# Output projections with tokens on partitions, and norms handed on in pieces of one and two k-tiles

## The reference

```python
def layer_norm(x, g, b):
    mu = jnp.mean(xf, axis=-1, keepdims=True)
    var = jnp.mean(jnp.square(xf - mu), axis=-1, keepdims=True)
    return (xf - mu) * lax.rsqrt(var + LN_EPS) * g + b
...
        x = layer_norm(ALPHA * x + mix, ln1_g[layer], ln1_b[layer])            # mix = ... @ w_out
        x = layer_norm(ALPHA * x + conv_ffn(x, ...), ln2_g[layer], ln2_b[layer])  # ... @ w_down
...
        h = rms_norm_2(x, ln_pre_g[layer])
        proj = jnp.einsum('bsd,de->bse', h, w_in[layer])
...
        y = jnp.einsum('bsd,de->bse', merged, w_o[layer])
        x = x + rms_norm_2(y, ln_post_g[layer])
```

## Time and profile before

| | |
|---|---|
| median of 3 runs | 3606.42 us (3606.31 to 3611.41) |
| profiled execution, its own time | 3607.19 us |
| its span (first to last instruction) | 3605.3 us |
| TensorE matmuls, share of the span | 3450.6 us, 96% |
| DVE, ACT, POOL | 64%, 40%, 11% |
| granted TensorE clock, mean | 0.985 of full |

### The profile page before, as it was taken

The page is one execution under the profiler, slowest core; times in us unless marked ns, Lnnn a source line. Parts: engine busy times, 40 slices in busy tenths (PEclk is TensorE's granted clock), DMA queues, the critical chain, the costliest instruction groups (busy, mean ns, idle before and its releaser), DMA issues.

```text
span 3605.3 us, 48876 instructions
## 1 busy us (share of the span) xinstructions
PE 3450.6 (96%) x19568; PEld 2980.7 (83%) x19568; DVE 2311.8 (64%) x2199; ACT 1428.3 (40%) x1113; POOL 405.9 (11%) x240
## 2 busy tenths in 40 slices
PE   8999899999999999899999999989999899999997
PEld 7888788888888888688888888878788788788886
DVE  5754667788874466467888874458766556545666
ACT  5542344333333345444333333345533333343332
POOL 0400130111111101030111111100000000000002
PEclk9999899999999999999999999999999999999999
DMA  5444144554555544144555455534444434435543
GB/s 209 172 175 145 71 161 175 186 184 179 184 186 187 186 146 172 59 164 168 182 185 186 179 183 192 187 131 155 162 177 181 145 140 175 152 134 185 183 179 135
DMA packets 84065, 598.16 MB, mean 166 GB/s; under 512 B 9329, under 2 KB 10481, under 8 KB 12146
## 3 DMA queue, kind: packets, MB, share of 16 engines
q1 hardware_dynamic: 81216, 589.34, 45.3%
q10 hardware_dynamic: 2738, 7.23, 0.6%
HBM read 594.43 MB, written 2.10 MB: 165 GB/s over the span
## 4 chain that ended last, share of the span: by engine, by line
PE 66%; issue 19%; DVE 7%; ACT 3%; POOLq 2%; POOL 1%; DVEq 1%; DMA 0%; ACTq 0%
PE acc L263 38%; PE acc L262 20%; DVE w_lo L192 4%; PE acc L259 3%; ACT w_hi L188 2%; POOLq L346 2%; PE acc L260 1%; PE acc L1431 1%; POOL over L344 1%; PE acc L1482 0%; DVE u_tiles L283 0%; PE acc L360 0%; PE acc L386 0%; DVE over L283 0%; POOLq L730 0%
## 5 line engine op out<-in xcount | busy, mean ns | idle before, releaser
L263 PE MATMUL acc<-x_hi_lo,w_hi 128*128 128x512 f32 x6720 | 2367.9, 396 | 0.0
L192 DVE TENSOR_TENSOR w_lo<-w_raw,w_hi 128x2048 fp32r<-128x2048 f32 x560 | 1387.6, 2478 | 1096.5 <-ACT w_hi L188 1095.1
L262 PE MATMUL acc<-x_hi_lo,w_lo 128*128 128x256 f32 x6720 | 1894.8, 282 | 15.5 <-DVE w_lo L192 15.5
L188 ACT ACTIVATE w_hi<-w_raw 128x2048 fp32r<-128x2048 f32 x560 | 1073.0, 1916 | 1963.2 <-PE acc L263 1963.2
L263 PEld LDWEIGHTS acc<-x_hi_lo,w_hi 128*128 128x128 f32 x6720 | 1266.1, 188 | 297.6 <-issue 4.1
L262 PEld LDWEIGHTS acc<-x_hi_lo,w_lo 128*128 128x128 f32 x6720 | 1273.0, 189 | 31.1 <-DVE w_lo L192 12.2
L263 PE MATMUL acc<-hidden_hi_lo,w_hi 128*128 128x512 f32 x1728 | 604.4, 395 | 0.0
L262 PE MATMUL acc<-hidden_hi_lo,w_lo 128*128 128x256 f32 x1728 | 482.2, 279 | 3.5 <-DVE w_lo L192 3.5
L263 PEld LDWEIGHTS acc<-hidden_hi_lo,w_hi 128*128 128x128 f32 x1728 | 324.2, 188 | 76.3
L262 PEld LDWEIGHTS acc<-hidden_hi_lo,w_lo 128*128 128x128 f32 x1728 | 325.3, 188 | 5.2 <-DVE w_lo L192 4.4
L259 PE MATMUL acc<-x_hi_lo,w_hi 128*128 128x512 f32 x448 | 169.1, 410 | 48.0 <-DVE w_lo L192 32.7
(11 more groups left out here) (250 smaller groups left out, 1685.7 us busy)
## 6 DMA issues: line engine op xcount, KB each, us to landing
w_raw<-weights_dram SPq DMA_DIRECT2D x560, 1024.0 KB, 4.8
resid<-x_dram ACTq DMA_DIRECT2D x4, 512.0 KB, 10.3
over<-w_gates_dram ACTq DMA_DIRECT2D x1, 2048.0 KB, 7.4
out_dram<-resid SPq DMA_DIRECT2D x4, 512.0 KB, 2.7
over<-con_dram ACTq DMA_DIRECT2D x5, 128.0 KB, 2.4
par<-par_dram ACTq DMA_DIRECT2D x1, 525.0 KB, 12.2
over<-con_dram ACTq DMA_DIRECT2D x2, 256.0 KB, 7.3
over<-gmlp_ws_dram ACTq DMA_DIRECT2D x1, 512.0 KB
```

What stands on the lines that cost most here:

```text
L188: nc.scalar.activation(whi[:, slot, :], raw[:, slot, :], ACT.Copy).then_inc(weights_hi, 1)
L192: nc.vector.tensor_tensor(wlo[:, slot, :], raw[:, slot, :], whi[:, slot, :].bitcast(F32), ALU.subtract).then_inc(weights_split, 1)
L262: nc.tensor.matmul(*rest, start=False, stop=False)
L263: last = nc.tensor.matmul(*both, start=False, stop=(k == CK * nch - 1))
```

## The change

In the five stages of `BY_TOKEN` the roles in the product are exchanged (`multiply_by_token`): a block of 128 tokens of the activations is loaded, hi or lo, and the weights stream past it, 512 output columns at a time, so that a bank holds 128 tokens by 512 features. Three matmuls of 512 columns (hi x hi, hi x lo, lo x hi) take the place of two pairs. A task uses two banks, one for each block `b` of tokens; in its last chunk all of block 0 comes first and is announced by `block_done`. The residual is kept token-major too (`z`: 128 x 2 x 2048), x is loaded a second time in that form, and gain and bias of the norms come as rows written to all partitions (`load_row`). Moments of a token are then sums along the free axis: `bn_stats` for each 512 features, `bn_aggr` at the end, a root on ACT for one column and a reciprocal. The affine step is two scalar_tensor_tensor on the DVE. The next stage needs feature-major input: TensorE transposes pieces (`GROUPS`: two of one k-tile and seven of two) into PSUM banks 4 to 7, ACT makes the hi part from there, the DVE the lo part, and TensorE waits for each piece by itself within the first task (`turn_before`). POOL no longer takes part in the norms. In last_out ACT squares the banks with an accumulated sum, the DVE multiplies by the gain row, and at the end one operation scales and adds for each 512 features, stored in eight parts. Since pieces of the norm run on ACT and the DVE, the split of the next stage's second chunk is moved to behind group 3 (`hold`).

```diff
+GROUPS = [(0,), (1,)] + [(k, k + 1) for k in range(2, MT, 2)]
+NGROUP = len(GROUPS)
...
+BY_TOKEN = ("mix0_out", "down0", "attn_out", "down1", "last_out")
+BLOCK0 = {n: 4 * i for i, n in enumerate(BY_TOKEN)}
+FEEDS = {"mix0_out": ("up0", 0), "down0": ("attn_in", 1), "attn_out": ("up1", 2), "down1": ("rnn_in", 3)}
...
-                            if not isinstance(n, int) or n + 2 < NCHUNKS:
+                            if not (last and hold) and (not isinstance(n, int) or n + 2 < NCHUNKS):
...
+                            if first and c < nch - 1 and f == 0:
+                                before_k(k)
...
+        def multiply_by_token(pe, name, moving, ready=None, cuts=(), banks_read=None):
...
+                        if c < nch - 1:
+                            places = [(b, kk) for kk in range(CK) for b in range(2)]
+                        else:
+                            places = [(b, kk) for b in range(2) for kk in range(CK)]
+                        for b, kk in places:
+                            bank, k = 4 * t + b, CK * c + kk
+                            w_hi, w_lo = (w[:, s, kk * CF * P:(kk + 1) * CF * P] for w in (whi, wlo))
+                            x_hi_b, x_lo_b = (moving(k, at0 + b * P, at0 + (b + 1) * P) for at0 in (0, T))
+                            nc.tensor.matmul(acc[:, bank, :], x_hi_b, w_hi, start=(k == 0), stop=False)
+                            nc.tensor.matmul(acc[:, bank, :], x_hi_b, w_lo, start=False, stop=False)
+                            last = nc.tensor.matmul(acc[:, bank, :], x_lo_b, w_hi, start=False,
+                                                    stop=(k == CK * nch - 1))
+                            if k == CK * nch - 1 and b == 0:
+                                last.then_inc(block_done, 1)
+                        last.then_inc(chunk_used, 1)
...
+        def wait_block(eng, name, q, b, n):
+            if b == 0:
+                eng.wait_ge(block_done, BLOCK0[name] + q + 1)
+            else:
+                eng.wait_ge(chunk_used, n + 1)
...
+        def affine(dve, b, at0, n):
+            zp = part(b, at0, n)
+            dve.scalar_tensor_tensor(zp, zp, moments[:, b, 0:1], row_g[:, at0:at0 + n], ALU.subtract, ALU.mult)
+            dve.drain()
+            return dve.scalar_tensor_tensor(zp, zp, rst[:, b:b + 1], row_b[:, at0:at0 + n], ALU.mult, ALU.add)
...
+        def group_scale(dve, g):
+            at0, n = group_cols(g)
+            for b in range(2):
+                o = dve.scalar_tensor_tensor(u_tok[:, b, at0:at0 + n], part(b, at0, n), rst[:, b:b + 1],
+                                             pre_row[:, at0:at0 + n], ALU.mult, ALU.mult)
+            o.then_inc(x_tok, 1)
...
+        def dve_residual(name):
...
+                for b in range(2):
+                    zp = part(b, 512 * q, 512)
+                    wait_block(dve, name, q, b, n)
+                    o = dve.scalar_tensor_tensor(zp, zp, ALPHA, acc[:, 4 * t + b, :], ALU.mult, ALU.add)
+                    if b:
+                        o.then_inc(acc_free, 1)
+                    dve.drain()
+                    dve.bn_stats(stats[:, b, q, :], zp)
+                    if q == 3:
+                        dve.drain()
+                        dve.bn_aggr(moments[:, b, :], stats[:, b].rearrange("p q s -> p (q s)")).then_inc(ln_var, 1)
+                        if b == 0:
+                            dve.wait_ge(rows_landed, 16 * (2 * occ + 2))
+                        dve_rstd(dve, 2 * occ + b + 1, b)
+                        if name == "down1":
+                            dve_pre_affine(dve, b)
+                        elif b == 0:
+                            affine(dve, 0, *group_cols(0))
+                        else:
+                            affine(dve, 1, *group_cols(0)).then_inc(x_tok, 1)
...
+        def dve_pre_affine(dve, b):
             for q in range(4):
+                affine(dve, b, 512 * q, 512).then_inc(z_norm, 1)
...
+        def group_lo(dve, nxt, g):
+            k0, n = GROUPS[g][0], len(GROUPS[g])
+            dve.wait_ge(x_hi, READY0[nxt] + g + 1)
+            dst = xhl[:, k0:k0 + n, :]
+            dve.tensor_tensor(dst[:, :, T:2 * T], acc[:, 4 + g % 4, 0:n * T].rearrange("p (k n) -> p k n", k=n),
+                              dst[:, :, 0:T].bitcast(F32), ALU.subtract).then_inc(moving_ready, 1)
+        def group_hi(act, nxt, g):
+            k0, n = GROUPS[g][0], len(GROUPS[g])
+            act.wait_ge(turned, NGROUP * FED_BY[nxt][1] + g + 1)
+            act.activation(xhl[:, k0:k0 + n, 0:T], acc[:, 4 + g % 4, 0:n * T].rearrange("p (k n) -> p k n", k=n),
+                           ACT.Copy).then_inc(x_hi, 1)
+        def group_turn(pe, nxt, g):
+            occ = FED_BY[nxt][1]
+            src = u_tok if nxt == "rnn_in" else z
+            pe.wait_ge(x_tok, NGROUP * occ + g + 1)
+            for at0, k in enumerate(GROUPS[g]):
+                for b in range(2):
+                    o = pe.transpose(acc[:, 4 + g % 4, at0 * T + b * P:at0 * T + (b + 1) * P],
+                                     src[:, b, k * P:(k + 1) * P], ident[:])
+            o.then_inc(turned, 1)
+        def turn_before(pe, nxt):
+            def before_k(k):
+                for g, ks in enumerate(GROUPS):
+                    if ks[0] == k:
+                        if g + 1 < NGROUP:
+                            group_turn(pe, nxt, g + 1)
+                        pe.wait_ge(moving_ready, READY0[nxt] + g + 1)
+            return before_k
+        def norm_pe(pe, nxt):
+            keep_clock(pe, 24)
+            group_turn(pe, nxt, 0)
+        def norm_dve(dve, name):
+            nxt = FEEDS[name][0]
+            go = group_affine
+            if name == "down1":
+                dve.wait_ge(pre_landed, 16)
+                dve.wait_ge(squares, 8)
+                dve.tensor_reduce(moments[:, :, 0], parts[:], AX, ALU.add).then_inc(ln_var, 1)
+                dve_rstd(dve, 9, 0, 2)
+                go = group_scale
+                go(dve, 0)
+            for g in (1, 2, 3):
+                go(dve, g)
+                group_lo(dve, nxt, g - 1)
+            split_chunk(dve, CHUNK0[nxt] + 1, 1)
+            for g in (4, 5):
+                go(dve, g)
+                group_lo(dve, nxt, g - 1)
+        def norm_act(act, name):
...
+            root(0)
+            act.wait_ge(raw_landed[slot], 16 * (n // 2 + 1))
+            act.wait_ge(chunk_used, n - 1)
+            act.activation(whi[:, slot, 0:CHUNK // 2], raw[:, slot, 0:CHUNK // 2], ACT.Copy)
+            root(1)
+            act.activation(whi[:, slot, CHUNK // 2:CHUNK], raw[:, slot, CHUNK // 2:CHUNK], ACT.Copy)\
+               .then_inc(weights_hi, 1)
+            if name == "down1":
+                for b in range(2):
+                    for q in range(4):
+                        act.wait_ge(z_norm, 4 * b + q + 1)
+                        act.activation(pre_squares[:, b, 512 * q:512 * q + 512], part(b, 512 * q, 512), ACT.Square,
+                                       accum_out=parts[:, b, q:q + 1]).then_inc(squares, 1)
+                act.wait_ge(ln_var, 9)
+                act.activation(std[:], moments[:, :, 0], ACT.Sqrt, bias=eps[:, 1:2], scale=1.0 / DM).then_inc(ln_std, 1)
+            for g in range(5):
+                group_hi(act, nxt, g)
...
+                if isinstance(i, int) and (i, t, c) == (0, 0, 2):
+                    go(dve, 8)
+                    group_lo(dve, name, 7)
+                    group_lo(dve, name, 8)
...
+        def act_last(i, t, task, n):
+            act, q = nc.scalar, 2 * i + t
+            for b in range(2):
+                wait_block(act, "last_out", q, b, n)
+                act.activation(last_squares[:, b, 512 * q:512 * q + 512], acc[:, 4 * t + b, :], ACT.Square,
+                               accum_out=parts[:, b, q:q + 1])\
+                   .then_inc(squares, 1)
+                if q == 3:
+                    act.wait_ge(ln_var, 10 + b)
+                    act.activation(std[:, b:b + 1], moments[:, b, 0:1], ACT.Sqrt, bias=eps[:, 1:2], scale=1.0 / DM)\
+                       .then_inc(ln_std, 1)
         def dve_last(i, t, task, n):
...
+            for b in range(2):
+                dve.wait_ge(squares, 8 + 2 * q + b + 1)
+                if q == 3:
+                    dve.tensor_reduce(moments[:, b, 0:1], parts[:, b, :], AX, ALU.add).then_inc(ln_var, 1)
+                o = dve.tensor_tensor(y_tok[:, b, 512 * q:512 * q + 512], acc[:, 4 * t + b, :],
+                                      post_row[:, 512 * q:512 * q + 512], ALU.mult)
+                if b:
                     o.then_inc(acc_free, 1)
                 if q == 3:
+                    if b:
+                        final_parts(dve, 0, (2, 3))
+                    dve_rstd(dve, 10 + b, b)
+                    final_parts(dve, b, range(4) if b else range(2))
+        def final_parts(dve, b, quarters):
+            for q in quarters:
+                zp = part(b, 512 * q, 512)
```

(2 more changed lines are left out.)

437 lines of the change are left out of this document (175 added, 262 removed).

## The result

The changed kernel takes **3568.76 us** (median of 4 runs, 3563.19 to 3569.56) where the kernel before, in the same comparison, takes 3607.89: a ratio of 0.9887, 95% interval 0.9870 to 0.9904. That is 39 us or 1.1% less. Timed once more beside the first experiments it gave 3566.02 (4 runs, 3558.46 to 3573.72) and a ratio of 0.9864 (0.9842 to 0.9887). The profiled execution took 3569.56 us, with a span of 3567.7.

The account below looks back on a forecast made before the run. TensorE, busy 96%, was taken as the bound, so only chunk time and joints could matter. Stream 0, layer-norm joints -6, rnn_in -15 and tail -14 sum to -35 on 3606.4, giving 3571 us; range 3554 to 3590.

Parts of the forecast that it names:

- The stream: Main matmuls of the five token-major stages, 136 chunks: same columns, same 5.67 us a chunk, change 0, bounds -20 to +12.
- Rival (a): All-512 streaming in the five stages is faster: 53 us more gained, 3518, or 3504 by the skill's figure; chance 0.06.
- rival (c): The five streams get slower through activation-block loads: 11 ns a step cancels the gain, 20 ns gives 3636; chance 0.05.
- rival (b): Joints give back more, by slower bn_stats or 1.2 GHz in last chunks: 5 us at three, 4 at rnn_in, 3590; 0.13.
- Rival (d): The early start at the joints is void because a raw chunk or gain rows come late: 3580; chance 0.06.
- The layer-norm joints: Into up0, attn_in, up1: first matmul at 7.3 us, then DVE-bound, 38.1 against 40.7; 3 x -2 = -6 in all.
- The rnn_in joint: Last matmul to the next stage's second task: first matmul at 19.2, 47 us against 62, -15, bounds -18 and -12.
- The tail: From the last matmul to the end of the span: 10.6 us against 24.7, -14, bounds -15 and -12.
- What costs nothing: DVE work per task, and loads of gain rows and x's token copy beside half-busy transfers, were put at 0.

Follow-up runs that it names:

- s_256: The changed kernel with nearly every 512-column matmul of the five token-major streams cut into two of 256 columns: 3602.2 us, ratio 0.9970.
- the control: The changed kernel itself, unedited, timed again beside the follow-up variants: 3566.02 us, ratio 0.9864 to the kernel before.
- j_onepass: The changed kernel with gain and bias left out after the first group in the three layer-norm joints: 3546.7 us.
- j_order: The changed kernel with ACT's attention constant loads, and the recurrent stage's gate-weight load and Exp, issued one chunk later: 3561.26 us, ratio 0.9859.
- j_kmajor: The changed kernel with the last chunk of the first task after each of four joints run k-tile by k-tile: 3558.65 us, ratio 0.9849.
- both_fill: The kernel of both, with 45 small matmuls without use added in the rnn_in joint: 3553.66 us, ratio 0.9844.
- both: The changed kernel with the edits of j_kmajor and j_order together: 3558.63 us, ratio 0.9858.
- j_nofill: The changed kernel without the 24 small matmuls without use behind each of four streams: 3565.28 us, ratio 0.9872.

## Why the prediction was right, and where it was wrong

The forecast of 3571 is 2 us from the measured 3568.8, and faster was rightly near certain. The sum was closer than its terms.

- **The stream: the term was mis-sized, 0 against -15.8.** I had the row that decides: 512 behind 512 is 557.32 to 557.55, 0.23, and I wrote it down. Then I took two thirds of a pair, 0.2365, with the reason that steps go by columns. They don't: 768 columns at 2.4 GHz are 320 ns, and a pair takes 27 or 33 ns more, by the task's pace; after, a step is 213.3 + 13.3 to 13.6. Eight matmuls fewer a chunk at 13.3 ns, the cost that s_256 shows by itself, are 0.107 us, over 136 chunks -14.5. That is the whole distance to the faster pace before. The slower pace, in 77 chunks, makes another -8.2; no run shows why a task ran at one pace or the other, so this part is measured and not explained. Of the -22.7 together, 6.9 are lost again in waits and slow clock inside the streams: 3 beside the transfers of the gain and bias rows, 1.6 through a spell of 3.4 us at the start of last_out that the control does not have, the rest in small pieces. So -14.5 lies near -15.8 by luck. The bounds (-20 to +12) held the sum, since they went by the rounding of the rows; the pace alone lies outside them.
- **Rival (a)** and **rival (c)** are both excluded: the step is 227 ns, not 220 and not 247. Loads of the activation blocks did not show. The Trainium skill (TensorE: Matmul & The Clock Gate, "Back-to-back issue gap") has 216 ns a step, 2.5 over the columns; this kernel shows 13.3 to 13.6 over them, and the measurement decides. Of **rival (b)** the second half came true, a spell at 1.2 GHz in the last chunk of a first task, at 1.5 us in two joints and not 5 in three. **Rival (d)** is out, with the first matmuls at 7.3; its gain and bias rows were late for no joint, but their transfers did hold up weights inside two streams. Two of the forecast's figures do not follow from its terms: 5 us lost give 3576 for (d) and not 3580, and -18 -9 -15 with a fifth of -20 is -46, a lower bound of 3560 and not 3554. The measured time lies inside either range.
- **The layer-norm joints: the mechanism was right, -6 against -1.1.** First matmul at 7.3, as forecast; the DVE's queue gives most of the rest back, as forecast, and j_onepass shows that it does. Into up0 it was -1.8 for -2. In attn_in I had not followed ACT's queue: three loads issued ahead of a cast put it off by 1.5 us (j_order). In attn_in and up1 a spell of 3.4 us at 1.2 GHz hits the last chunk, and it is not hidden there, since that chunk decides when the next task starts: 1.5 us each (the difference between j_kmajor's gains with and without it). I had allowed 0.6.
- **The rnn_in joint: -11.6 against -15.** First matmul at 20.4 for 19.2, of which slow transposes at 1.2 GHz are 0.25 (both_fill). I had put the clock at 2, and it is 1.9. The largest term that I left out is TensorE's own transposes between the matmuls of the first task. In both_fill, at the full clock and without a wait, its second and third chunk take 6.50 and 6.46 us where a chunk without transposes takes 5.55 to 5.65; over four chunks that is some 3.4 us beyond my 22.6. The gap before the fourth chunk was forecast at 3 and is 3.5. It is made of the waiting for group 8 as a whole, 1.5 (j_kmajor), and of ACT's queue with the gate weights' load and the Exp's table, 1.2 (j_order); with both edits it is gone. These pieces overlap, so they add up to more than the 3.4 us missed.
- **The tail: -15.65 against -14.** The DVE ends 6.57 us after the last matmul's start for 6.2; from there to the end of the span it takes 2.5 us instead of the 4.4 that I had carried over, because the last store lands 2.1 us after its issue; before, the last two stores of 512 KB were issued one right behind the other and the last took 3.6. The table load of 1.28 is hidden.
- **"What costs nothing" cost 6.5, of which 4.2 are the first attention stage of the last layer.** Between half0's and half1's first matmul 277.7 us instead of 273.4. The rows of 25 us there, kernel after, and the same place in j_kmajor:

```profile
2860.00:2885.00 25.00, 20.99 (x110) 18.59 (x110) 6.79 (x10) 7.62 (x12) 0.00 (x0) 0.80 0.00 1
```

```profile
2854.00:2879.00 25.00, 21.52 (x133) 18.72 (x132) 7.69 (x8) 8.84 (x11) 0.00 (x0) 1.00 0.12 43
```

With the same code there, j_kmajor has no such spell of 10.2 us at 1.2 GHz and needs 273.5; j_order, both and j_nofill lie between (274.3 to 275.9). The length of this stage goes with its time at 1.2 GHz: 3.4 us of it for 273.5, 10.2 for 275.9, 16 for 277.7. But the changed kernel has 277.7 in both of its profiles, and s_256 too, so it is not chance from one execution to the next. What in the stages ahead decides where the clock falls in this stretch with gaps stays open. The remaining 2.3 us are spread over other stages and were not followed up.

## What to carry to other kernels

Count matmuls as well as columns: taking the same columns in fewer, longer matmuls was worth some 13 ns for each matmul saved between 256 and 512 columns here, and far more below. A new load that goes "beside" the weights can still hold up a weight chunk: look for it in the stream, not only at the joint. An early first matmul is worth only what the queue behind it lets through, so sum that queue to the next task's start, with every instruction that another engine has ahead of the piece that is awaited. Before moving work to an idle engine, ask whether the two can run at once at all.

## What the runs showed of the hardware that was not expected

- Step of a fp32r matmul at the full clock: 227 ns for 512 columns, 120 for 256, and 112 for 128. Halving the columns again saves 8 ns.
- A shared stationary block saves nothing: 227 ns between matmuls with the same one and with another, and a load is recorded for each.
- A DVE step with two SBUF tensors stood still for up to 4.1 us (4.43 instead of 0.35) until GpSimd's instruction ended; steps with one SBUF tensor beside it kept their time to 0.01 us.
- Pairs of 512 and 256 columns ran at one of two paces through a whole task, 5.55 or 5.65 us a chunk, both at the full clock; matmuls of 512 columns alone had one pace, 5.44.
- 6.8 us at 1.2 GHz cost 0.6 in a joint where TensorE waits for the DVE, 3.4 us cost 1.5 in a chunk that decides when the next task starts.
